# Attention block: ScalarE writes the first output weights' high part in front of the last query's eviction

## The reference

```python
q = (h @ w_q).reshape(b, s, N_BRANCHES, N_HEADS, HEAD_DIM)
outs, lses = [], []
for g, (window, dil) in enumerate(BRANCHES):
    o, l = _dilated_branch(q[:, :, g], kv[:, :, 0, g], kv[:, :, 1, g], window, dil, slopes[g])
    outs.append(o)
    lses.append(l)
wts = jax.nn.softmax(jnp.stack(lses, axis=0), axis=0)
o = jnp.sum(wts[..., None] * jnp.stack(outs, axis=0).astype(jnp.float32), axis=0)
return o.reshape(b, s, D_ATTN).astype(h.dtype) @ w_o
```

## Time and profile before

| what | value |
|---|---|
| timed runs, median of 3 | 1310.19 us (1309.7 to 1317.32) |
| the profiled execution | 1307.66 us, its span 1305.9 us |
| PE busy | 1254.2 us, 96% of the span |
| POOL busy | 846.8 us, 65% |
| ACT busy | 653.2 us, 50% |
| DVE busy | 601.3 us, 46% |
| mean DMA | 186 GB/s, 242.76 MB |
| mean granted TensorE clock | 0.983 of full speed |

### The profile page before, as it was taken

One profiled execution on the slowest core, in us unless ns is written; L12 is line 12 of the kernel. 1 busy time (PEld: TensorE's weight loads), 2 busy tenths in 40 slices (PEclk: granted clock), 3 DMA queues, 4 the chain that ended last, 5 costly groups with the idle time before them and its releaser, 6 DMA issues.

```text
span 1305.9 us, 24860 instructions
## 1 busy us (share of the span) xinstructions
PE 1254.2 (96%) x10093; PEld 1119.7 (86%) x10093; DVE 601.3 (46%) x1369; ACT 653.2 (50%) x1074; POOL 846.8 (65%) x445
## 2 busy tenths in 40 slices
PE   6997988889999999999999999999999999999998
PEld 6993547679899999999988889998988789988887
DVE  6658687642676695432555512412111114555411
ACT  5531343125755554654666643656554554655642
POOL 8984500025788877664788777667765655888782
PEclk8998999989999999999999999999999999999999
DMA  8859895603465555435555566443648893455550
GB/s 263 214 169 376 316 343 209 212 29 102 158 194 177 171 178 186 162 129 162 161 191 183 175 194 194 130 147 113 194 134 262 266 294 120 160 189 193 178 177 33
DMA packets 232943, 242.76 MB, mean 186 GB/s; under 512 B 9196, under 2 KB 201854, under 8 KB 232830
## 3 DMA queue, kind: packets, MB, share of 16 engines
q1 hardware_dynamic: 232510, 241.08, 57.0%
q10 hardware_dynamic: 320, 0.10, 0.0%
HBM read 240.11 MB, written 1.05 MB: 185 GB/s over the span
## 4 chain that ended last, share of the span: by engine, by line
PE 80%; DVE 5%; ACT 2%; issue 1%; POOL 1%; DMA 0%; DVEq 0%; SPq 0%; ACTq 0%
PE banks L572 79%; DVE arena L1804 1%; DVE banks L1804 1%; DVE arena L1797 1%; PE banks L1428 1%; ACT ring_hi L2569 1%; POOL ring_lo L1716 1%; ACT arena L2569 1%; DVE hn_lo L1804 1%; DMA ring<-in_w_kv_dram 0%; DVE banks L1797 0%; DVE arena L1810 0%; PE banks L582 0%; PE banks L914 0%; PE banks L1037 0%
## 5 line engine op out<-in xcount | busy, mean ns | idle before, releaser
L1716 POOL TENSOR_TENSOR ring_lo<-ring,ring_hi 128x2048 fp32r<-128x2048 f32 (+1 forms) x176 | 717.1, 4090 | 393.4 <-ACT ring_hi L2569 392.9
L2569 ACT ACTIVATE ring_hi<-ring 128x2048 fp32r<-128x2048 f32 (+1 forms) x176 | 300.1, 1706 | 113.0 <-PE banks L572 70.2
L572 PE MATMUL banks<-hn_hi,ring_lo 128*128 128x256 f32 x1160 | 321.1, 284 | 0.0
L572 PE MATMUL banks<-hn_hi,ring_hi 128*128 128x256 f32 x992 | 279.7, 288 | 7.0 <-ACT hn_hi L2569 3.1
L2569 ACT ACTIVATE arena<-banks 128x256 f32<-128x256 f32 (+6 forms) x350 | 134.2, 399 | 275.9 <-PE banks L572 212.8
L572 PE MATMUL banks<-hn_lo,ring_hi 128*128 128x256 f32 x992 | 257.5, 284 | 0.0
L572 PEld LDWEIGHTS banks<-hn_hi,ring_lo 128*128 128x128 f32 x1160 | 221.9, 192 | 0.1
L572 PEld LDWEIGHTS banks<-hn_hi,ring_hi 128*128 128x128 f32 x992 | 191.5, 193 | 10.7 <-issue 4.4
L572 PE MATMUL banks<-hn_pair,ring_hi 128*128 128x512 f32 (+1 forms) x768 | 183.4, 374 | 0.1
L572 PEld LDWEIGHTS banks<-hn_lo,ring_hi 128*128 128x128 f32 x992 | 180.5, 193 | 0.1
L572 PEld LDWEIGHTS banks<-arena 64*32 64x32 f32 (+6 forms) x1698 | 108.8, 155 | 63.8 <-issue 39.5
(11 more groups left out here) (286 smaller groups left out, 1909.5 us busy)
## 6 DMA issues: line engine op xcount, KB each, us to landing
ring<-in_ada_w_dram SPq DMA_DIRECT2D x48, 1024.0 KB, 9.1
ring<-in_ffn_w_up_dram SPq DMA_DIRECT2D x44, 1024.0 KB, 5.2
ring<-in_w_up_dram SPq DMA_DIRECT2D x22, 1024.0 KB, 5.2
ring<-in_w_kv_dram SPq DMA_DIRECT2D x34, 512.0 KB, 4.3
ring<-in_ffn_w_down_dram SPq DMA_DIRECT2D x16, 1024.0 KB, 5.3
ring<-in_w_in_dram SPq DMA_DIRECT2D x9, 1024.0 KB, 8.2
ring<-in_attn_w_q_dram SPq DMA_DIRECT2D x18, 512.0 KB, 4.0
ring<-in_kv_ada_w_dram SPq DMA_DIRECT2D x8, 1024.0 KB, 7.0
```

The costliest lines, as they stand in the source:

```text
L572: return nc.tensor.matmul(o, l, r, start=start, stop=stop, **k)
L1716: led.emit(g.tensor_tensor(low, raw, high.bitcast(F32), ALU.subtract), sem("lo_ready"))
L2569: led.emit(nc.scalar.activation(o, x, func, **k), signal, value)
```

## The change

The last query (c = 3, br = 2, i = 1) is now evicted with `take` instead of `take0`, so that `reach` is called in front of its eviction.

```diff
             def queries_out(c, br, i):
-                b = take0(("dq", c, br, i)) if (c, i) == (3, 1) else take(("dq", c, br, i))
+                b = take0(("dq", c, br, i)) if (c, i) == (3, 1) and br < 2 else take(("dq", c, br, i))
                 af(shaped(dq[:, c % 2, 2 * br + i, :], 2, 4, 32), query_order(b[:, 0:T], 2), ACT.Identity, *freed(("dq", c, br, i)), scale=0.125)
```

## The result

Timed in 18 runs each, the changed kernel takes 1318.17 us (median) and the kernel before 1309.92: the ratio of the two sets of runs is 1.0057, 95% interval 1.0039 to 1.0074, that is 7.5 us slower (5.1 to 9.7). The direction and the mechanism were forecast, the size (+3.6, with a range up to 1317.2) was not: it is twice that. A later measurement, with 8 and 25 runs, gave 1.0060 (1.0036 to 1.0083).

What follows compares the result with a forecast made beforehand. TensorE was taken as the bound. Scores 5.27 us later less the old 2.26 us wait gave +3.0, the clock +0.55, about +3.6 in all: 1310.19 + 3.6 = 1313.8 us, range 1310.8 to 1317.2.

Steps and rivals of the forecast that it cites:

- Steps 1 and 2: ScalarE's last-query eviction starts at 1073.47 behind three high parts; TensorE's step 14 scores start about 1073.9, 5.27 us later.
- step 3: Before TensorE's output matmuls: earlier low parts remove the old 2.26 us wait, leaving a net +3.0 us.
- Step 5: TensorE's clock after the new wait: slow stretch costs 2.2 us instead of 1.65, so +0.55 us.
- My upper case, +4.8: Rival, chance 0.25: TensorE's slow stretch of 6.8 us lies all over work, +4.8 us, time 1315.0.
- The rule of the Trainium skill: Cited for the long-slow-stretch rival (+4.8 us, chance 0.25): TensorE out of a longer hole starts slow for certain.
- The 425 GB/s of the Trainium skill: Output-weight transfers: a chunk would take 2.47 us, the sum without the clock about +0.8; set aside for the trace.
- The faster rival: Chunks landed early, so ScalarE's high parts run back to back and the clock holds: −2.1 us, 1308.1; chance 0.04.

Runs made afterwards that it cites:

- one_ahead: Only the first output-weight chunk's high part put in front of the last query's eviction, against the kernel before: ratio 0.9981, measured again 0.9983.
- two_ahead: High parts of the first two output-weight chunks put in front of the last query's eviction, against the kernel before: ratio 1.0014.
- dve_after: The changed kernel with VectorE instead of ScalarE evicting the last query, the three high parts left where they were: ratio 1.0009 against the kernel before.
- after_dense_first: The changed kernel with 32 extra constant matmuls between the wait for the last query and the scores of step 14: half speed 6.8 us, scores of step 15 at 24.71 us.

## Why the prediction was wrong

- **The mechanism, right.** The eviction waits for do2's transfer, the scores of step 14 for the eviction, the wait for `hn_lo` disappears, low parts and sums stay hidden, and beyond the place TensorE carries the delay to the end. one_ahead, two_ahead and dve_after show the steps apart.
- **Steps 1 and 2, the start of the scores: +5.27 forecast, +6.07 measured.** do2's high part began 8.15 us after the second-last eviction (forecast 7.66), since its transfer took 7.8 us and ScalarE started 0.36 us behind the landing (1077.55 in the chain); and from the eviction's start to the scores it was 0.72 us, not the 0.43 I had put. That moves the net wait of step 3 from 3.0 to 6.07 - 2.26 = 3.81. The prediction took the start of do2's high part in the kernel before, 1071.67, for a sign of the landing; it is only the end of do1's high part, and says no more than that the chunk was there. do0 came late too (its transfer took 10.5 us, not 9.1, and its high part began 2.00 us after the second-last eviction, not 0.59), which cost nothing.
- **Step 5, the clock: +0.55 forecast, +3.76 measured; the step that failed.** Half speed cost 6.15 - 3.59 = 2.56 us in the block and 7.17 - 4.32 = 2.85 in the output matmuls, together 5.41 where the prediction took 2.2, less the 1.65 of before. I had bounded the cost at 3.4 us, half of a slow stretch of 6.8 us, the longest one I had read in the trace of before, and had taken its length to be set by the hole. In the traces it goes by what follows the hole: through the small matmuls the clock stayed at 0.50. My upper case, +4.8, fell with the same bound. 3.81 + 3.76 = 7.57, the whole of the place in this profile; the other two profiles of the changed kernel give 4.13 + 2.95 and 4.07 + 2.55.
- **The rule of the Trainium skill** that I had made a rival ("TensorE: Matmul & The Clock Gate", "What's actually happening": the slow clock is the default and activity releases it) pointed to this side, and the traces agree so far: TensorE came out of the hole at 0.50. But it then stood at 0.50 over 6.20 us in which it was busy 6.15 us by the profile.
- **The 425 GB/s of the Trainium skill** ("DMA: Bandwidth & Descriptors", "Bandwidth"), which the prediction set against the trace, are the table's row for 16 MB; its row for 1 MB, the size of a chunk, has 341 GB/s, and the trace's 344 to 352 are close to that. The landings were taken from the trace, so nothing hung on it.
- **What a measurement can tell** was put at 1%, some 13 us. The 18 runs of each kernel told 0.57% from nothing, with an interval of 0.18% to each side.
- **The faster rival** had its mechanism right too (early high parts shorten the old wait and save the clock). Its condition, do2 landed by then, was not met, but do0 alone is enough for it: that is one_ahead.

What stays open: the prediction was made from one trace of before, in which everything up to the place ran 0.6 to 8.8 us earlier than in the other profiles; why that early part varies was not tried. How much of the slow stretch falls into the hole also differs between the three profiles of the changed kernel (1.4 to 4.1 us of 13.6 to 13.7), and what sets it is not shown.

## What to carry to other kernels

An instruction of an in-order engine that waits for a transfer takes everything behind it along: put such copies in front of a short eviction only when their data have landed by then, one at a time and not all that are allowed to go. Price a new hole on TensorE by its length and by what stands behind it: before small matmuls the half-speed stretch was two to three times as long as before dense ones, and in the changed kernel it added 2.55 to 3.76 us to the 3.81 to 4.13 us of waiting. Filling the hole with constant matmuls held the clock, and what stood behind them started within 0.1 us of where it had (the scores of step 14 at 10.76 against 10.69 us, the output matmuls at 10.54 against 10.47).

## What was not expected of the hardware

- At half speed TensorE can be busy almost without a gap and stay there: 12.3, 10.4 and 9.5 us in the three profiles of the changed kernel, in the first of them over matmuls of 64 rows or 32 and 64 columns, transposes and then 29 full ones. Behind a hole of like length, with full matmuls alone, full speed was back in about 5 us (after_dense_first).
- VectorE's subtraction of two SBUF tensors beside a running subtraction of GpSimd took 4.30 us instead of 0.42, and the profile of before holds the same case, unread by me: a VectorE row on 128x8 elements of 4.58 us beside GpSimd's low parts. The Trainium skill says so ("SBUF — State Buffer", "SBUF: two separate sides": the port pair that both engines share is locked for a whole instruction, by VectorE when it has two SBUF inputs and the GpSimd instruction reads SBUF), and the trace agrees: that row ends at 1083.47, where the second of the three low parts of the earlier trace rows ends (1074.34 + 2 x 4.56 = 1083.46). The row of VectorE in the timeline of before:

```profile
1078.89 4.58 DVE L1804 SCALAR_TENSOR_TENSOR gsc<-mod,par 128x8 f32<-128x8 f32 x1
```
